# Turning the softmax weights of a head at two steps of the attention loop instead of three, and v's blocks one step earlier

## The reference, cut to what matters

```
for blk in range(s // Q_BLOCK):
    ...
    scores = jnp.einsum('bqhmd,bkhmd->bhmqk', qb, kb,
                        preferred_element_type=f32)
    ...
    probs = jax.nn.softmax(scores + bias[None, :, None], axis=-1)
    weights = probs[:, :, 0] - lam * probs[:, :, 1]
    outs.append(jnp.einsum('bhqk,bkhe->bqhe', weights.astype(v.dtype), vb))
o = jnp.concatenate(outs, axis=1)
o = rms_norm(o, head_norm_g) * (1.0 - lam_0)
```

## Time and profile before

| | us |
|---|---|
| median of 3 runs (1896.51 to 1899.50) | 1897.87 |
| the profiled execution, its own time | 1898.01 |
| its span | 1896.2 |

### The profile page before, as it was taken

How to read it: one execution, slowest core, us unless ns; L and a number is a source line. 1 busy time by engine, 2 the same in 40 slices (tenths; PEclk the granted TensorE clock), 3 DMA queues, 4 the chain that set the end, 5 groups by cost and what they waited for, 6 DMA issues and landing times.

```text
span 1896.2 us, 22387 instructions
## 1 busy us (share of the span) xinstructions
PE 1868.0 (99%) x8923; PEld 1450.5 (76%) x8923; DVE 996.8 (53%) x1778; ACT 817.9 (43%) x1328; POOL 123.8 (7%) x148
## 2 busy tenths in 40 slices
PE   8999999999999999999999999999999999999997
PEld 6566666666788788888886777778888878888886
DVE  6667666666544653333346667845434763333322
ACT  6566656656633342222323655434432442222221
POOL 0111111110001000000010011000000100000000
PEclk9999999999999999999999999999999999999999
DMA  5444343432233232222333323221123323233331
GB/s 199 164 145 156 144 145 145 145 145 101 78 129 117 67 111 100 93 96 94 100 86 125 99 70 106 68 94 35 45 89 111 124 92 102 94 100 97 92 95 61
DMA packets 56526, 201.95 MB, mean 107 GB/s; under 512 B 6478, under 2 KB 6934, under 8 KB 55784
## 3 DMA queue, kind: packets, MB, share of 16 engines
q1 hardware_dynamic: 44616, 158.32, 25.3%
q0 software_dynamic: 11808, 42.21, 6.1%
HBM read 195.23 MB, written 5.28 MB: 106 GB/s over the span
## 4 chain that ended last, share of the span: by engine, by line
PE 87%; DVE 6%; ACT 4%; issue 1%; DMA 0%; SPq 0%; DVEq 0%; ACTq 0%
PE ps L1204 25%; PE ps L1207 24%; PE ps L1205 24%; PE ps L1304 2%; PE ps L1268 2%; PE ps L1340 1%; ACT wH L1910 1%; PE ps L1292 1%; DVE wL L1499 1%; PE ps L1280 1%; ACT a L2009 1%; DVE a L1622 1%; PE ps L1347 1%; PE ps L1257 1%; DVE g1a L1499 1%
## 5 line engine op out<-in xcount | busy, mean ns | idle before, releaser
L1204 PE MATMUL ps<-hH,wH 128*128 128x512 f32 (+1 forms) x1560 | 634.8, 407 | 1.0 <-DVE hL L1570 1.0
L1207 PE MATMUL ps<-hH,wL 128*128 128x512 f32 (+1 forms) x1560 | 610.7, 391 | 1.0 <-DVE wL L1499 0.7
L1205 PE MATMUL ps<-hL,wH 128*128 128x512 f32 (+1 forms) x1560 | 609.0, 390 | 0.0
L1499 DVE TENSOR_TENSOR wL<-wr,wH 128x1024 fp32r<-128x1024 f32 (+2 forms) x285 | 343.9, 1207 | 483.8 <-ACT wH L1910 483.2
L1910 ACT ACTIVATE wH<-wr 128x1024 fp32r<-128x1024 f32 (+2 forms) x285 | 295.1, 1036 | 233.3 <-PE ps L1207 218.3
L1204 PEld LDWEIGHTS ps<-hH,wH 128*128 128x128 f32 (+1 forms) x1560 | 292.7, 188 | 93.6 <-issue 32.4
L1207 PEld LDWEIGHTS ps<-hH,wL 128*128 128x128 f32 (+1 forms) x1560 | 292.3, 187 | 66.9 <-DVE wL L1499 3.9
L1205 PEld LDWEIGHTS ps<-hL,wH 128*128 128x128 f32 (+1 forms) x1560 | 293.1, 188 | 61.3 <-issue 6.5
L1204 PE MATMUL ps<-gffn,wH 128*128 128x512 f32 x400 | 157.0, 393 | 1.0 <-DVE xT L1677 0.9
L1205 PE MATMUL ps<-gffn,wH 128*128 128x512 f32 x400 | 155.8, 390 | 0.0
L1207 PE MATMUL ps<-gffn,wL 128*128 128x512 f32 x400 | 155.8, 390 | 0.0
(11 more groups left out here) (304 smaller groups left out, 2079.9 us busy)
## 6 DMA issues: line engine op xcount, KB each, us to landing
wr<-wst SPq DMA_DIRECT2D x268, 512.0 KB, 3.4
a<-wfd POOLq DMA_DIRECT2D x54, 512.0 KB, 5.0
xT<-wfd POOLq DMA_DIRECT2D x18, 512.0 KB, 6.9
wr<-wst SPq DMA_DIRECT2D x16, 384.0 KB, 3.0
xT<-xin SPq DMA_DIRECT2D x8, 256.0 KB, 6.8
xT<-xin SPq DMA_DIRECT2D x2, 1024.0 KB, 7.0
xsave<-xT SPq DMA_DIRECT2D x1, 2048.0 KB, 7.3
c<-wfd POOLq DMA_DIRECT2D x8, 256.0 KB, 3.7
```

The source lines that it names most:

```text
L1204: e.matmul(o, hi, xh[k], start=k == 0, stop=False)
L1205: e.matmul(o, hi, xl[k], start=False, stop=False)
L1207: i = e.matmul(o, lo, xh[k], start=False, stop=k == t.nk - 1)
L1499: e.tensor_tensor(dst, x, hi.bitcast(F32), ALU.subtract).then_inc(s[name], 1)
```

## The change

Three numbers of the table change: `vturn` goes from step 10 to step 9, and the four `turnw` from steps 4, 7, 7, 13 to steps 7, 7, 14, 14. Nothing is added and nothing removed.

```
-SCHED = {"rstd": 1, "v": 10, ... "d": [4, 7, 7, 13], "pv": 18, "ada": 30,
+SCHED = {"rstd": 1, "v": 9, ... "d": [7, 7, 14, 14], "pv": 18, "ada": 30,
```

More of the change, by code:

```diff
@@ L70, in shape_constants @@
     return c
-SCHED = {"rstd": 1, "v": 10, "table": 2, "c": [(9, (0, 1)), (14, (2,)), (18, (3,))], "w": [11, 12, 16, 21],
-         "c0": [(14, (0, 1)), (17, (2,)), (20, (3,))], "w0": [16, 17, 19, 22], "d": [4, 7, 7, 13], "pv": 18, "ada": 30,
+SCHED = {"rstd": 1, "v": 9, "table": 2, "c": [(9, (0, 1)), (14, (2,)), (18, (3,))], "w": [11, 12, 16, 21],
+         "c0": [(14, (0, 1)), (17, (2,)), (20, (3,))], "w0": [16, 17, 19, 22], "d": [7, 7, 14, 14], "pv": 18, "ada": 30,
          "o": 5, "lo": (12, 18)}
```

## The result

| | us |
|---|---|
| before, median of 4 runs (1896.51 to 1900.83) | 1898.68 |
| after, median of 4 runs (1916.92 to 1920.87) | 1919.15 |
| the profiled execution after, its own time | 1920.75 |
| its span | 1919.0 |

The ratio of after to before is 1.0113, 95% interval 1.0101 to 1.0125: 1.1% slower, as forecast (1919).

A forecast was written before the change was run, and what follows sets the result against it. TensorE, busy 99% of the span, was taken as the bound. Costs of 10.9, 4.0, 5.4 and 1.0 us sum to 21.3, taking 1898.0 to 1919 us; its own range 1914 to 1924, 8 in 10 within 1908 to 1930.

The forecast's parts named there:

- v's turn and its bank: Step 9, passes 2 to 16: v's turn waits 1.47 us for ScalarE's copy of kb = 0, 15 times.
- The shift in a pass: TensorE within a pass: scores of block 2 start 1.45 us late, everything after step 14's transpositions 1.8 us late.
- Passes behind `ada` at step 9: Six passes (3, 8, 9, 10, 15, 16): nothing of the new wait is absorbed, 1.82 us each, 10.9 us.
- the ends: Passes 16, 2 and 17: +1.7 us, less 0.45 and some 0.3 for turns lost, together +1.0 us.
- Passes behind `ada` at 14 and 18: Four passes each: step-5 lateness absorbs part of the shift, leaving 1.0 us each (4.0) and 1.36 each (5.4).
- S: Lateness of the sum of o at step 5 from standing or waiting since step 4: 0.81, 1.36 or 0.44 us.
- The reading of the earlier trace: Step 4, line 1280: the turn of kb = 0 waits for ScalarE's Ln of q, 8.8 us at 16 places.
- The reading of "issue": Step 5: 6.1 us idle at 12 places before the sum of o is a wait for VectorE's line 1499.
- Costed at nothing: VectorE's copies of v and kb = 3, and `pv` at step 18: no cost; `pv` 0.4 us a pass if uncovered.
- The first: Rival: step-5 waits absorb more in six passes behind `ada` at step 9, 0.44 us each; 1911 us; 15%.
- The second: Rival: v's wait at step 9 does not come, leaving only gains; 1887 us; 4%.
- The third: Rival: the clock falls in the new waits, once a pass at 1.7 us, 26 us more; 1945 us; 14%.

The follow-up runs named there:

- e3: The changed kernel with the turn of kb = 0 at step 5 instead of 7, v's turn still at step 9; 1901.59 us, 1.0023 of the kernel before.
- e6: The changed kernel with the `ada` units that stood at step 9 moved, so all stand at step 14 or 18; 1916.50 us, 1.0096 of the kernel before.
- e4: The kernel before with VectorE's low part of o's squares moved from step 0 to step 22 of the pass before; 1894.86 us, ratio 0.9987.
- e2: The kernel before with only the weights' turns moved, to steps 7, 7, 14, 14, v's turn left at step 10; 1900.09 us, ratio 1.0004.
- e9: The kernel before with o's low part at step 22, v-tile weight split later, `ada` off step 9 except in passes 3 and 10; 1892.50 us, ratio 0.9971.
- e10: e9 with the weights' turns at steps 7, 7, 14, 14 and v's turn left at step 10; 1890.25 us, 0.9962 of the kernel before.
- e5: The kernel before with the `ada` units that stood at step 9 moved, so all stand at step 14 or 18; 1898.39 us, ratio 1.0004.

## Why the prediction was right, point by point

- **v's turn and its bank.** Forecast 1.47 at 15 places for ScalarE's copy; 1.46 in pass 13, 15 places. e3 shows that the late copy of its bank makes it: with the turn of kb = 0 two steps sooner the wait is gone with v's turn in the same place and on the same bank.
- **The shift in a pass.** Forecast 1.45 at the scores of block 2 and 1.8 at the end. v's turn, its wait and the first scores take 3.02 between stream matmuls in pass 13, against 1.52 before for scores and v's turn apart (+1.50); step 7 with seven transpositions 0.78, and its four before 0.56 (+0.22); the single one of step 13 saves 0.12; scores and three transpositions at step 14 take 1.34 against 1.06 (+0.28). The sum is 1.88.
- **Passes behind `ada` at step 9.** Forecast 1.82 each, and a wait of 1.4 at the sum of o; 1.76 to 1.87 in five of the six, and six waits of 1.2, or 1.35 by starts (1.58 less the 0.23 of the grid). Pass 3 is the sixth, at 1.35: its missing turn at step 4 was priced under the ends. e6 shows the class from the other side: with these passes gone the waits are gone too, and the change costs 4.1 less.
- **Passes behind `ada` at 14 and 18.** Forecast 1.0 and 1.36; 1.07 to 1.11, and 1.41 twice and 1.24 twice. That all of S is absorbed shows in step 5 of pass 13 above. The shift of 1.88 less the S of 0.81 in pass 13 is 1.07. I had priced four passes as pass 11; two of them have a larger S.
- **The ends.** Forecast +1.0. Pass 17 grows by 1.45, and pass 3 by 0.47 less than the 1.82 of its class: +0.98.
- **The reading of the earlier trace rows.** The prediction has the 8.8 us on weight loads at 16 places. They are 10 places: 6.3 us are of ten weight loads, and 2.5 are of the matmuls behind six of the same. No term of the sum was taken from this number.
- **The reading of "issue".** S was taken to end with VectorE's line 1499 although the trace named no engine. e4 showed it by moving that one instruction.
- **Costed at nothing.** VectorE's copy of v, its copy of kb = 3 and `pv` show no wait of TensorE in the changed kernel, which agrees. Behind pass 17 another 0.19 us came in at the sum of o of pass 18, which had no term.
- **The rivals.** The first had the passes behind `ada` at step 9 at 0.44; it falls by the 1.76 to 1.87. The second falls by the 15 waits. The third, a fall of the clock in the new waits, falls too: in no stretch of 1 us between 64 and 520 us is the granted clock after under 1.00. By the rival's price of 1.7 us, 15 falls would bring the mean of an execution to some 0.987, and the four executions after show 0.997 to 0.999. The second of the waits (pass 3), and the stretch behind it:

```profile
102.00:103.00 1.00, 0.00 (x0) 0.00 (x0) 0.40 (x1) 1.00 (x3) 0.00 (x0) 1.00 0.00 0
103.00:104.00 1.00, 0.89 (x8) 0.73 (x10) 1.00 (x2) 0.43 (x2) 0.00 (x0) 1.00 0.00 0
```

The prediction's own ground for this was weaker than it looked. It took the stop of 1.5 us near 1286 us, behind which the clock stayed at 1.00, as the like case. In the profiles of e2, e4 and e9 the clock did fall behind this same stop, and the 39.9 us from there to the first transposition of line 1436 became 41.4; in the other nine profiles it stayed up. e4, where the two have lines 1407 and 1439:

```profile
1281.76 0.22 PE L1407 MATMUL ps<-a 32*32 32x32 f32 x2 [1.50 <-DVE a L1841]
```

```profile
1283.00:1286.00 3.00, 3.00 (x10) 2.42 (x8) 1.37 (x2) 0.59 (x1) 0.00 (x0) 0.50 0.02 5
```

So a stop of 1.5 us can be followed by a fall in this kernel, and that one trace showed none there was luck. That the 15 waits brought none is shown by the runs, and not by that comparison.

The rule that the prediction weighed by the Trainium skill (TensorE: Matmul & The Clock Gate, Part 4: PE-mode transpose), that transpositions don't count as busy for the clock gate in the way that matmuls do, would have made a fall likelier; in this kernel, with 4 transpositions right behind a wait of 1.46, 7 more two steps ahead of it, and a stream around them, no fall was seen. The runs do not test the rule by itself.

The prediction's sum was hit to 0.3 us, the sizes of its terms to within 0.5. That the median also agrees so closely (1919.15) is in part luck: the profiled executions are 22.7 apart, of which 0.7 came in ahead of the change.

## What to carry to other kernels

Where several kinds of work take buffers from one ring in turn, moving a piece by one place changes whose reader it waits for: write down, for each taker, who read the buffer last and when that reader is through. A new wait on an in-order engine costs its own length less the lateness that it meets further on; so look for where the engine is late next, and for what that place hangs on, since a chain that itself starts from the delayed engine absorbs nothing. Idle time that a trace puts down to no one may still be a semaphore wait: move the instruction that ends just ahead of it and see.

## What the runs showed that I had not expected

Between 55 and 60 us TensorE waits 1.9 to 2.6 us for VectorE's line 1622 in every one of these kernels. In some executions the granted clock then falls to half, 1.2 GHz, and in others it stays at 2.4. The kernel before, answering to the earlier trace rows in other windows:

```profile
59.00:61.00 2.00, 2.00 (x7) 0.83 (x4) 1.89 (x6) 0.91 (x4) 0.00 (x0) 0.50 0.62 252
```

and e10:

```profile
59.00:61.00 2.00, 2.00 (x10) 1.61 (x9) 1.89 (x6) 0.88 (x4) 0.00 (x0) 1.00 0.86 350
```

In the profiles of e3, e4, e5 and e10 it stayed up, in the other eight it fell. Step 1 of pass 2 came 1.6 to 1.9 us sooner in these four than in the kernel before, about what the prediction priced one fall at (1.7); at step 1 of pass 3 0.8 to 1.6 of it were left. Before, e4 and e5 have the same instructions up to this wait, so this is a difference between executions and not between kernels. It is of the size of the difference between e9 and e10 (2.25 in the medians). The profile of e9 has both falls, this one and the one near 1280 us, and that of e10 neither. Of e10's five executions the two with a mean granted clock of 0.998 took 1887.80 and 1888.26, the three with 0.997 took 1890.25 to 1891.44, and all eight of e9 show 0.997. So a good part of what e10 seems to gain on e9 may be the clock. What decides on a fall is not settled by these runs. For small gains the growth from pass to pass behind this point is therefore the better measure than the span.
